# A PEER layer on one Trainium2 core: another order of the accumulator additions, and 15 row gathers a group in place of 16

## The reference, cut to what matters

```
act = gelu(einsum('td,thkd->thk', tc, u_emb[ec]))
out = einsum('thk,thkd->td', act * gc, v_emb[ec])      # gc: softmax gates
h = h + out;  return rmsnorm(h, g_final)
```

## Time and profile before

| what | value |
|---|---|
| median of 3 runs | 3320.5 us (3315.7 to 3323.35) |
| profiled execution, its own time | 3315.37 us |
| its span, first to last instruction | 3313.6 us |
| PE busy | 3005.1 us (91%) |
| DVE busy | 2215.5 us (67%) |
| POOL busy | 1219.7 us (37%) |
| mean granted PE clock | 0.975 |

### The profile page before, as it was taken

One profiled execution on the slowest core, in us unless ns is written; L12 is line 12 of the kernel. 1 busy time (PEld: TensorE's weight loads), 2 busy tenths in 40 slices (PEclk: granted clock), 3 DMA queues, 4 the chain that ended last, 5 costly groups with the idle time before them and its releaser, 6 DMA issues.

```text
span 3313.6 us, 53097 instructions
## 1 busy us (share of the span) xinstructions
PE 3005.1 (91%) x20010; PEld 2447.0 (74%) x20010; DVE 2215.5 (67%) x5340; ACT 1009.9 (30%) x1487; POOL 1219.7 (37%) x1072
## 2 busy tenths in 40 slices
PE   8997989996999866689999999999999999999997
PEld 4444666545777666678988888888888888888876
DVE  2223544336898889868887777777777777777445
ACT  2223555312233278722221122222222221222212
POOL 0000000001222300023357767666666676675241
PEclk9998999998999989999999999999999999999998
DMA  5213111112111126797799999999999999999684
GB/s 190 99 65 117 38 46 33 47 45 99 59 57 56 48 64 182 242 308 267 255 324 386 380 368 383 384 372 387 381 381 379 378 389 374 390 377 343 225 323 168
DMA packets 330176, 779.27 MB, mean 235 GB/s; under 512 B 45648, under 2 KB 147280, under 8 KB 328528
## 3 DMA queue, kind: packets, MB, share of 16 engines
q0 software_dynamic: 129024, 469.82, 37.8%
q1 hardware_dynamic: 178512, 288.92, 24.9%
q10 hardware_dynamic: 22400, 17.32, 1.6%
HBM read 699.42 MB, written 72.35 MB: 233 GB/s over the span
## 4 chain that ended last, share of the span: by engine, by line
PE 45%; DVE 9%; DMA 5%; issue 3%; ACT 1%; POOL 1%; SPq 0%; DVEq 0%; ACTq 0%
PE psum L1890 21%; PE psum L1906 19%; PE psum L1932 5%; DVE first L1575 4%; DMA u_ring<-u_rows,eid 3%; DVE one L1568 1%; DMA scr_g<-gates 1%; DVE acc L2095 1%; DVE u_lo L2059 1%; POOL v_ring L1863 1%; ACT u_hi L1987 1%; DVE second L1578 1%; DMA v_ring<-v_rows,eidT 1%; DVE w_lo L2076 0%; DMA v_raw<-v_rows 0%
## 5 line engine op out<-in xcount | busy, mean ns | idle before, releaser
L1863 POOL DMA_INDIRECT v_ring<-v_rows,eidT x448 | 593.6, 1325 | 413.0 <-PE psum L1932 303.4
L1855 POOL DMA_INDIRECT u_ring<-u_rows,eid x448 | 513.0, 1145 | 302.1 <-DVE dots L2103 199.8
L2103 DVE CUSTOM_DVE_ANT_0 u_ring<-u_ring,rows 128x1024 f32<-128x1024 f32 x448 | 545.3, 1219 | 100.9 <-DMA u_ring<-u_rows,eid 99.6
L1890 PE MATMUL psum<-hn_hi_e,u_hi 128*128 128x288 f32 x1792 | 530.2, 296 | 8.9 <-PEq L107 5.5
L1906 PE MATMUL psum<-w_hi,v_hi 128*128 128x288 f32 x2048 | 466.7, 310 | 71.5 <-DVE acc L2095 60.4
L1890 PE MATMUL psum<-hn_lo_e,u_hi 128*128 128x288 f32 x1792 | 528.0, 295 | 0.0
L1890 PE MATMUL psum<-hn_hi_e,u_lo 128*128 128x288 f32 x1792 | 527.7, 294 | 0.0
L2095 DVE TENSOR_TENSOR acc<-psum,acc 128x576 f32<-128x576 f32 x504 | 380.3, 755 | 143.4 <-PE psum L1906 133.2
L1906 PEld LDWEIGHTS psum<-w_hi,v_hi 128*128 128x128 f32 x2048 | 335.1, 194 | 175.0 <-issue 93.2
L1906 PE MATMUL psum<-w_lo,v_hi 128*128 128x288 f32 x2048 | 447.4, 301 | 0.0
L1906 PE MATMUL psum<-w_hi,v_lo 128*128 128x288 f32 x2048 | 447.1, 301 | 0.0
(11 more groups left out here) (243 smaller groups left out, 4232.4 us busy)
## 6 DMA issues: line engine op xcount, KB each, us to landing
v_raw<-v_rows SPq DMA_DIRECT2D x128, 512.0 KB, 7.0
u_raw<-uT SPq DMA_DIRECT2D x112, 512.0 KB, 8.1
w<-scr_g SPq DMA_DIRECT2D x128, 288.0 KB, 5.9
scr_g<-gates SPq DMA_DIRECT2D x3, 8192.0 KB, 30.8
scr_m<-st_m SPq DMA_DIRECT2D x8, 1024.0 KB, 4.0
w_raw<-in_w_pq SPq DMA_DIRECT2D x8, 1024.0 KB, 6.4
u_raw_r<-uT SPq DMA_DIRECT2D x16, 512.0 KB, 3.5
scr_g<-gates ACTq DMA_DIRECT2D x1, 7680.0 KB, 36.1
```

Of the source, the lines that this page charges most:

```text
L1855: pool.indirect_dma_start(u_ring[:, n % U_RING, :], None, core.i["u_rows"], bass.IndirectOffsetOnAxis(eid[:, x // 2, x % 2, k:k + 1], 0)). ...
L1863: pool.indirect_dma_start(v_ring[:, m % V_RING, :], None, core.i["v_rows"], bass.IndirectOffsetOnAxis(eidT[:, x // 2, col:col + 1], 0)).th ...
L1890: last = nc.tensor.matmul(ps[:, a, 0:COLS], x[:, c, j, :], y[:, j, a * COLS:(a + 1) * COLS], start=m == 0, stop=m == len(terms) - 1)
L2103: nc.vector.tensor_tensor_reduce(out=u, in0=u, in1=rows[:, x % 2, :], scale=1.0, scalar=0.0, op0=ALU.mult, op1=ALU.add, accum_out=dots[:, ...
```

## The change

In `plan`, while u rows remain, a group has eight u rows and seven v rows instead of eight and eight, except that the first v group of each unit keeps eight v rows. Once all u rows are done, every group may take 16 v rows, the first one of a unit as well. The iterations in `TURN` go from 9, 17, 25, 33, 41, 49, 57 to 9, 17, 26, 35, 44, 53, 59, and those that close units from 18, 26, 34, 42, 50, 57, 63 to 19, 28, 37, 46, 55, 60, 64 (64 is behind the loop). Before, the last v rows belonged to group 62; after, they belong to group 63.

On DVE, `add(g, 0)` comes right behind `gated(g + 1, 0)` (and a unit's `close`), and the two splits stand between the additions 0, 1 and 2. The same is done in the second half with the additions 4, 5 and the splits of c = 1. The dots move a little: the third one goes from behind addition 0 to behind addition 2, and three stand together ahead of the second gating.

```
-ROWS_A_GROUP, MOST_DOTS, LAST_ROWS = 16, 9, 16
+U_ROWS, MOST_DOTS, LAST_ROWS = 8, 9, 16
@@ plan
-        nv = min(ready, LAST_ROWS if u == total and v % UNIT else 8)
-        nu = min(total - u, ROWS_A_GROUP - nv, MOST_DOTS)
+        nv = min(ready, LAST_ROWS if u == total else 7 if v % UNIT else 8)
+        nu = min(total - u, U_ROWS if nv else MOST_DOTS)
@@ DVE, in the loop over g
                 gated(g + 1, 0)
-                split_u(g + 2, 0)
-                split_w(g + 1, 0)
                 for x in closes(g):
                     close(x)
                 add(g, 0)
+                split_u(g + 2, 0)
+                add(g, 1)
+                split_w(g + 1, 0)
+                add(g, 2)
                 some_dots(g, 3, 4)
-                add(g, 1)
-                add(g, 2)
-                some_dots(g, 4, 5)
                 add(g, 3)
                 for x in turns(g):
                     take_coef(g, x)
-                some_dots(g, 5, 7)
+                some_dots(g, 4, 7)
                 gated(g + 1, 1)
+                add(g, 4)
                 split_u(g + 2, 1)
+                add(g, 5)
                 split_w(g + 1, 1)
+                some_dots(g, 7, 8)
                 for x in closes(g - 1):
                     mean(x, False)
-                add(g, 4)
-                some_dots(g, 7, 8)
-                add(g, 5)
                 add(g, 6)
                 some_dots(g, 8, 9)
```

## The result

The changed kernel is slower: 3333.1 us median (3327.5 to 3339.9, 8 runs) against 3316.0 (3310.8 to 3323.4, 8 runs) for the kernel before, ratio 1.0057 with a 95% interval of 1.0044 to 1.007. The profiled execution has a span of 3329.5 us; the one of before has 3313.6. The forecast was 3290, its range ended at 3314.

What follows compares the result with a forecast made beforehand. The prediction took PE as the bound, with waits for DVE's additions. First stage -19, middle -10 and last groups 0 gave -29 us, from the median 3320.5 to 3291.5, put at 3290, range 3258 to 3314.

Steps and rivals of the forecast that it cites:

- First stage, -19: Iterations 1 to 10: additions ahead of splits end PE's waits in halves without a sum; -19 us, between -10 and -24.
- Short iterations by r: Iterations 12, 16, ... 52, each laid out from its start T; r is the rows before it modulo 4; together -4 us.
- r = 0: Three short iterations: addition 4 comes earlier, but the second sum is behind fill 7; fill 6 waits 3.0 us; gain 0.
- r = 2: Two short iterations: one sum only, dot 5 at T + 16, fill 6 waits 1.3 us; gain 3.3 us each.
- r = 3: Four short iterations: dot 5's row lands at T + 19, fill 6 waits 3.5 us; loss 0.4 us each.
- r = 1: Two short iterations: two gathers more are behind the sum, the row lands at T + 21; loss 0.5 us each.
- Closes and turns, -1.6: Middle: splits behind `close` gain 2.6 us in four full groups; the turn at iteration 44 costs 1.
- The lighter DMA load, -4.5: Middle: with 15 of 16 gathers rows land sooner, 0.5 us on nine short iterations; -4.5 us, between 0 and -22.
- The middle, -10: Short iterations with u rows, lighter DMA load, closes and turns together; -10 us, between -40 and +8.
- the freed middle: Middle: one row fewer ends the backlog, dot 5 lands sooner, nine short iterations gain 4 us; 3260 us; chance 0.25.
- Last groups, 0 within -5 to +8: Iterations 57 and 58 gain 4.9 us, iteration 63 with 16 rows costs net +5; 0, between -5 and +8.
- Slower: Seven iterations of r = 0 and 3: dot 5 comes behind T + 21, +28 us; 3319 to 3325 us; chance 0.08.

Runs made afterwards that it cites:

- the order alone: The change's DVE order with the row plan of the kernel before (eight u and eight v rows a group); 3260.5 us, ratio 0.9854.
- the shifted plan: The changed kernel with each unit's group of eight v rows at the unit's end instead of its start; 3314.2 us, ratio 1.0005.
- POOL's order one place earlier: The changed kernel with each u row issued one place earlier against its group's v rows; 3292.3 us, ratio 0.9946.

## Why the prediction was wrong

The steps that failed are three: ten sums of work that the sum left out of both places, the price of the last group, and 8.1 us to landing for a row wherever it is issued.

**First stage, -19: right.** It is 19.2 us shorter, and 18.1 by the order alone. Its waits fell from 31.2 to 12.0. A full iteration without sums (3, 6, 7) takes 26.28 us, two halves of 12.95 and 0.38 for DVE, which comes out late once a group as forecast. The prediction's own count there gives 12.46 us of DVE against 12.95, which would not be late.

**Short iterations by r: right for r = 0 and 2, mis-sized for 3 and 1, and these decide the middle.** r = 0: the prediction kept the wait; the three gained 3.2 in all, and in iteration 20 dot 5's row landed at T + 18.2, forecast T + 18.5. The chain there, of the changed kernel:

```profile
1993.08 8.59 DMA u_ring<-u_rows,eid
...
2004.32 4.98 PE psum L1906 x24
2009.29 1.85 PE psum L1932 x16
```

The iteration begins at 1983.42, and its second sum stands behind the fills, as laid out. r = 2: waits of 1.7 and 1.8, forecast 1.3. r = 3: the forecast was +0.4 each; the four waited 7.6 more in all, 1.9 each. In iteration 48 the row lands at T + 20.1, not T + 19; it is issued at T + 11.1, as laid out, and takes 8.94 us. r = 1: forecast +0.5 each, measured +7.5 and +9.0. The issue was laid out rightly, at T + 12.9 for a landing at T + 21; it came at T + 12.7 and T + 12.2. The landing failed: in the shifted plan r = 1 waits 9.3 and 10.1 us with 11.7 and 12.3 us to landing, without a slow load, and here such a load came on top, with 14.05 us in iteration 32 and 15.05 in 36:

```profile
2328.88 4.21 SPq L1787 DMA_DIRECT2D tail<-scr_h  x4
```

```profile
2335.00:2340.00 5.00, 5.00 (x41) 3.40 (x40) 0.64 (x1) 1.60 (x2) 3.29 (x4) 1.00 1.04 276
```

```profile
2335.41 1.90 PE psum L1932 x16
...
2337.57 0.94 POOL v_ring L1863
...
2338.81 0.94 POOL u_ring L1855
...
2340.05 1.35 POOL v_ring L1863
...
2341.70 14.05 DMA u_ring<-u_rows,eid
...
2357.69 0.68 DVE acc L2095
2358.41 5.61 PE psum L1906 x24
```

These are SP's issue, a window and the chain of iteration 32 of the changed kernel: the row is issued at T + 12.7 and lands 14.05 us later, at T + 26.7, where the prediction had T + 21. It took the 8.1 us to landing of the earlier trace rows for every place, and of SP's loads it looked at those of gates and u blocks only.

**Closes and turns, -1.6: right** where it can be read: the full iterations with a close (19, 37, 46, 55) wait for nothing, where those of before had 0.65 us.

**The lighter DMA load, -4.5: wrong.** In 1745 to 3040 the median time to landing of u rows did fall, from 8.3 to 7.7 us, but with 9.1 us the order alone is 52.8 us ahead in waits. A lower median bought nothing, for the rows that PE waits for are the late ones: where POOL stands, the share sinks (0.96), and then gathers go out in a row.

**The middle, -10: measured +0.5.** The prediction laid out the new order together with the new plan, against before, and so never had a price for either. By itself the order is worth -33.8 us in the middle, and the plan on top of it costs 34.3; their remainder was what I took for the worth of the change. The rival of the freed middle asked for one row fewer to bring this about; the order alone does it with all rows. The middle's ten sums fewer are worth 18.5 us of PE's work, which my sum counted neither here nor at the end, and waits eat them: +19.0 against before, +52.8 against the order alone. The signs that the prediction named as its refutation are all there: the middle's DMA share under 1.00 with landings at 7.7 us, full iterations that wait (18 for 4.8 us), and a last group over 10 us.

**Last groups, 0 within -5 to +8: measured +29.9.** This is the largest single miss. 18.5 is the work of ten sums, which the prediction let fill waits; with the new order there were none left to fill. Its list for the last group names two of them (3.7 us), but 2 + 2 + 3.5 + 3.7 - 1.9 - 0.7 is 8.6, and "net +5" is what comes out without them. The other 11.4 are waits, all in the last stretch. Its sums, from PE's timeline of the changed kernel (idle before in brackets):

```profile
3283.12 3.64 PE L1932 MATMUL psum<-v_ring,strip 128*32 128x512 f32 x16 [4.36 <-DMA v_ring<-v_rows,eidT]
3292.39 3.23 PE L1932 MATMUL psum<-v_ring,strip 128*32 128x512 f32 x16 [5.63 <-DMA v_ring<-v_rows,eidT]
3305.36 1.92 PE L1932 MATMUL psum<-v_ring,strip 128*32 128x512 f32 x16 [1.29 <-DMA v_ring<-v_rows,eidT]
```

With 1.50 us ahead of an earlier one they waited 12.8 us in all, where the prediction had 2, 2 and 3.5; and two of them ran at 3.64 and 3.23 us in place of 1.9. Behind the first of these waits the granted clock is 0.50:

```profile
3283.10:3286.80 3.70, 3.64 (x16) 0.67 (x16) 0.00 (x0) 0.00 (x0) 0.00 (x0) 0.50 1.03 410
```

Rounds of gather and sum were rightly named as the mechanism; the price was low by five microseconds for the waits and by three for the slower sums. The bound of +8 left the moved work out. With sixteen rows in the last group alone the price held (about 5 us); why the waits are longer where the groups ahead of it take sixteen each as well was not tested.

**The rivals.** "Slower" had the mechanism: u gathers behind v gathers that wait for a later sum. That POOL's order one place earlier takes back 41 us shows it. Its condition was wrong: it asked for landings behind T + 21 at r = 0 and 3, and the places are r = 1 and, by less, r = 3. Its time, 3319 to 3325, lies near 3333 by luck: it makes the middle 28 us longer than forecast where 10.5 were measured, and leaves out the end's 29.9. Against it I had held that in r = 3 the releasing sum comes earlier than before; it does, and seven gathers then go out ahead of the wanted one. "The freed middle" was true of the order and false of the whole.

**The start** of the expert stage lies 4.7 us later. Over these kernels, whose code up to there is the same, it lies anywhere from 1450.1 to 1457.4, so it is no part of the change.

**Open.** What fixes the start within these 7 us. What makes a row land 3.5 to 4 us late in r = 1 without a load beside it; gathers going out close together would fit, but nothing here tests it. Why one place earlier costs under the old plan. More buffers for v rows weren't tried.

## What to carry to other kernels

Price the parts of a change apart before pricing them together: here the order alone is worth 1.5%, and the plan that came with it costs more than that; and of the order, the additions and splits gain nothing until the dots are moved as well. Where one engine issues two kinds of gathers in order, each gather that waits for a consumer delays every one behind it: lay out which sum releases it at each place of a row count that no longer divides evenly, ask whose row is behind it, and take its time to landing from that place, not from a median. Work taken out of a stretch that another engine sets is not saved, but it is paid in full where it is put.

## What the runs showed of the hardware

A DMA share of 1.00 doesn't tell how much is moved. Beside two loads of rows into 64 partitions each (L1779), or four of 64 KB into 16 each (L1787), the share stays at 1.03 to 1.04 while the rate is 266 or 276 GB/s in place of 413, and the u rows issued beside them, as far as they are shown here, land after 12.2 to 15.1 us in place of 8.2. They carry no more bytes than one gather, and moved onto a short iteration of the order alone they cost it 3.6 to 7.5 us. What about them is slow, their width or their source or something else, was not tested. The Trainium skill ("DMA: Bandwidth & Descriptors", section "Back-pressure in remote DMA") says of transfers between cores that a saturated destination port holds up the engines that share its path; that would fit, but the loads here are not of that kind, and no run shows the ports. A row can be late at the full rate too: in iteration 44 of the shifted plan it took 12.32 us while the engines moved 409 GB/s.

The rates of 413 GB/s over five microseconds and 390 over 344 us lie above the 358 GB/s a core that the Trainium skill ("DMA: Bandwidth & Descriptors", section "Where 436 GB/s comes from") states for transfers between memory and the chip; the measurement decides. The page has its figure from dividing the rate of one memory stack by two cores, and this kernel runs on one core. The prediction gave up to 55 us for forty rows fewer if bytes were the bound; the middle without them gave back nothing for its bytes.

TensorE's clock: in iteration 44 of the order alone, where PE stood still 0.59 us ahead of fill 6, the granted clock stayed at 1.00, the 2.4 GHz level. After 2.93 us in iteration 20 of before the level fell to 1.2 GHz and 24 matmuls took 4.99 us. Behind a wait of 4.36 us in the changed kernel's last group it was 0.50, and a sum took 3.64 us in place of 1.92. So a shorter wait can give back more than its own length, though not always: iteration 36 of before kept its clock behind 2.99 us.
